# Two half-masked key blocks merged before the softmax, parted after the transpose; the pooling groups in every second step

## What is computed

```python
u_pool, q, k, v, gate_pool, gate_attn = jnp.split(hn @ w_in[l], SPLITS, axis=-1)
y_pool = pool_mixer(u_pool, pool_w_grp[l], pool_scale[l], w_pool_proj[l])
attn = swa_attention(q, k, v, sinks[l])            # 16 heads of 64, 4 key heads
merged = sigmoid(gate_pool) * y_pool + sigmoid(gate_attn) * (attn @ w_attn_proj[l])
h = h + rmsnorm(merged @ w_o[l], g[MIX_POST])
...
band_ok = (dist >= 0) & (dist < WINDOW) & (k_pos >= FRONT_PAD)     # WINDOW = 128
logits = concat([s_band - slope * dist where band_ok, s_meta, sink])
probs = softmax(logits); out = probs_band @ v + probs_meta @ v_meta
```

## Time and profile before

| | |
|---|---|
| time, median of 3 (range) | 1172.51 us (1171.82 to 1173.37) |
| the profiled execution's own time | 1172.02 us |
| its span, first to last instruction | 1170.2 us |
| TensorE busy | 1160.6 us, 99% |
| VectorE busy | 734.0 us, 63% |
| ScalarE busy | 554.6 us, 47% |
| GpSimd busy | 430.2 us, 37% |
| mean granted TensorE clock | 0.998 |

### The profile page before, as it was taken

How to read it: one execution, slowest core, us unless ns; L and a number is a source line. 1 busy time by engine, 2 the same in 40 slices (tenths; PEclk the granted TensorE clock), 3 DMA queues, 4 the chain that set the end, 5 groups by cost and what they waited for, 6 DMA issues and landing times.

```text
span 1170.2 us, 23880 instructions
## 1 busy us (share of the span) xinstructions
PE 1160.6 (99%) x9269; PEld 1133.2 (97%) x9269; DVE 734.0 (63%) x1145; ACT 554.6 (47%) x818; POOL 430.2 (37%) x486
## 2 busy tenths in 40 slices
PE   9999999999999999999999999999999999999997
PEld 8999999999999999999999999999999999999986
DVE  7655546968566865544586555459676668755542
ACT  7433335637554643333554333355376546543441
POOL 1945500007211286541109645000073122965500
PEclk9999999999999999999999999999999999999999
DMA  8854458372365365535646553573733753654540
GB/s 289 265 180 157 148 176 235 116 233 80 91 178 183 109 207 182 176 122 182 210 131 203 185 165 125 189 227 118 251 92 91 197 164 121 221 198 161 192 168 36
DMA packets 197934, 197.58 MB, mean 169 GB/s; under 512 B 4448, under 2 KB 191200, under 8 KB 197856
## 3 DMA queue, kind: packets, MB, share of 16 engines
q1 hardware_dynamic: 197712, 196.44, 53.3%
q10 hardware_dynamic: 144, 0.05, 0.0%
HBM read 195.43 MB, written 1.05 MB: 168 GB/s over the span
## 4 chain that ended last, share of the span: by engine, by line
PE 92%; issue 3%; DVE 2%; ACT 1%; DMA 0%; POOL 0%; SPq 0%; DVEq 0%; ACTq 0%; POOLq 0%
PE bank L563 27%; PE bank L565 27%; PE bank L564 27%; PE bank L826 2%; PE bank L828 2%; PE bank L827 2%; DVE w_lo L1347 1%; PE bank L915 1%; PE bank L910 1%; PE bank L869 1%; PE bank L599 1%; PE bank L598 1%; PE bank L880 1%; PE bank L626 0%; PE bank L872 0%
## 5 line engine op out<-in xcount | busy, mean ns | idle before, releaser
L563 PE MATMUL bank<-x_hi,w_hi 128*128 128x272 f32 (+1 forms) x1991 | 573.3, 288 | 0.8 <-DVE w_lo L1756 0.7
L565 PE MATMUL bank<-x_hi,w_lo 128*128 128x272 f32 (+1 forms) x1991 | 567.4, 285 | 0.0
L564 PE MATMUL bank<-x_lo,w_hi 128*128 128x272 f32 (+1 forms) x1991 | 566.3, 284 | 0.0
L1027 ACT ACTIVATE w_hi<-raw 128x2048 fp32r<-128x2048 f32 (+3 forms) x201 | 339.1, 1693 | 403.1 <-PE bank L565 383.5
L1347 DVE TENSOR_TENSOR w_lo<-raw,w_hi 128x2048 fp32r<-128x2048 f32 (+3 forms) x203 | 421.4, 2081 | 142.5 <-ACT w_hi L1027 142.2
L563 PEld LDWEIGHTS bank<-x_hi,w_hi 128*128 128x128 f32 x1991 | 374.9, 188 | 2.0 <-issue 1.2
L564 PEld LDWEIGHTS bank<-x_lo,w_hi 128*128 128x128 f32 x1991 | 375.6, 189 | 0.3
L565 PEld LDWEIGHTS bank<-x_hi,w_lo 128*128 128x128 f32 x1991 | 374.9, 188 | 0.0
L1968 POOL TENSOR_TENSOR hid_hi<-silu,up_r 128x272 f32 x88 | 142.1, 1615 | 149.3 <-DVE up_r L1543 143.2
L565 PE MATMUL bank<-hid_hi,w_lo 128*128 128x272 f32 x528 | 151.3, 287 | 0.0
L563 PE MATMUL bank<-hid_hi,w_hi 128*128 128x272 f32 x528 | 151.3, 287 | 0.0
(11 more groups left out here) (219 smaller groups left out, 1323.4 us busy)
## 6 DMA issues: line engine op xcount, KB each, us to landing
raw<-in_ffn_w_in SPq DMA_DIRECT2D x84, 1024.0 KB, 5.1
raw<-in_w_in SPq DMA_DIRECT2D x24, 1024.0 KB, 5.6
raw<-in_ffn_w_out SPq DMA_DIRECT2D x24, 768.0 KB, 4.2
raw<-in_ffn_w_out SPq DMA_DIRECT2D x24, 640.0 KB, 3.9
raw<-in_ffn_w_out SPq DMA_DIRECT2D x10, 1024.0 KB, 5.0
raw<-in_w_in SPq DMA_DIRECT2D x16, 512.0 KB, 5.4
raw<-in_w_attn_proj SPq DMA_DIRECT2D x32, 256.0 KB, 4.5
raw<-in_w_o SPq DMA_DIRECT2D x8, 1024.0 KB, 5.5
```

Of the source, the lines that this page charges most:

```text
L563: pe.matmul(ps[:, t0:T], w[0], a_hi[:, t0:T], start=start, stop=False)
L564: pe.matmul(ps[:, t0:T], w[0], a_lo[:, t0:T], start=False, stop=False)
L565: return pe.matmul(ps[:, t0:T], w[1], a_hi[:, t0:T], start=False, stop=stop)
L1027: last = act.activation(hi, w, ACT.Copy)
```

## The change

- The mask is laid on as before, and then VectorE takes, for the second block's queries, the minimum of the two key blocks' columns (they are held negated, so a masked entry is very large): one square of 128 by 128 in place of two half masked ones. `biased` is now incremented by this instruction; a new semaphore `banded` stands between.
- ScalarE's first exponential and GpSimd's first product take 144 and 128 columns in place of 272 and 256.
- `turn_p` makes two transposes of 128 by 128 in place of three, and `take_pT` copies 256 columns in place of 384.
- GpSimd, behind `pT_ready`, parts the turned square into the own block's and the earlier block's triangle with two `affine_select` (`cut_triangles`), and increments the new `pT_cut`. `attend` waits for `pT_cut` in place of `pT_ready`.
- The transposes of `p_meta` and of the spread values take 64 columns and not 128, those of the meta tokens' values 16; in layer 1 the latter are left out, with their copy.
- The pooling group g: window and mix in step 2g, group and take_z in step 2g+1. `attend_meta` moves from step 6 to step 7.

```diff
@@ turn_v
-                for j in range(2):
-                    pe.transpose(pTm_bank[:, j * P:(j + 1) * P], vT[:, j, 0:P], ident[:, :])
+                if meta_queries(l):
+                    for j in range(2):
+                        pe.transpose(pTm_bank[0:META, j * P:(j + 1) * P], vT[:, j, 0:META], ident[:, :])
@@ turn_p
-                pe.transpose(pT_bank[:, P:2 * P], s[:, META:META + P], ident[:, :])
-                last = pe.transpose(pT_bank[:, 2 * P:3 * P], s[:, META + P:T], ident[:, :])
+                last = pe.transpose(pT_bank[:, P:2 * P], s[:, META:META + P], ident[:, :])
...
-                    last = pe.transpose(pTm_bank[:, 0:P], p_meta[:, c:c + P], ident[:, :])
+                    last = pe.transpose(pTm_bank[0:4 * META, 0:P], p_meta[:, c:c + 4 * META], ident[:, :])
@@ attend
-                pe.wait_ge(pT_ready, l * HEADS + pair[1] + 1)
+                pe.wait_ge(pT_cut, l * HEADS + pair[1] + 1)
@@ TensorE's step
-                    if 1 <= c <= GROUPS:
-                        group(c - 1, l)
+                    if c % 2 == 1:
+                        group(c // 2, l)
@@ exps, take_pT
-                act.activation(s[:, 0:T], s[:, 0:T], ACT.Exp, scale=-1.0, bias=st[:, 2:3], accum_out=st[:, 4:5])
+                both = s[:, 0:META + P]
+                act.activation(both, both, ACT.Exp, scale=-1.0, bias=st[:, 2:3], accum_out=st[:, 4:5])
...
-                last = act.activation(pT[:, i % 2, :], pT_bank[:, 0:3 * P], ACT.Copy)
+                last = act.activation(pT[:, i % 2, 0:2 * P], pT_bank[:, 0:2 * P], ACT.Copy)
@@ bias_and_max
-                last.then_inc(biased, 1)
+                    if b == 0:
+                        last.then_inc(banded, 1)
+                dve.wait_ge(banded, n)
+                dve.tensor_tensor(s[:, META:META + P], s[:, META:META + P], s[:, META + P:T], ALU.min).then_inc(biased, 1)
@@ VectorE's step
-                    if 1 <= c <= GROUPS:
-                        take_z(c - 1, l)
+                    if c % 2 == 1:
+                        take_z(c // 2, l)
...
-                    if c < GROUPS:
-                        mix(c, l)
+                    if c % 2 == 0:
+                        mix(c // 2, l)
@@ GpSimd
+            def cut_triangles(i, l):
+
+                pool.wait_ge(pT_ready, l * HEADS + i + 1)
+                before, own = pT[:, i % 2, P:2 * P], pT[:, i % 2, 2 * P:3 * P]
+                pool.affine_select(out=own, in_=before, compare_op=ALU.is_ge, fill=0.0, base=0, pattern=[[1, P]],
+                                   channel_multiplier=-1)
+                pool.affine_select(out=before, in_=before, compare_op=ALU.is_ge, fill=0.0, base=-1, pattern=[[-1, P]],
+                                   channel_multiplier=1).then_inc(pT_cut, 1)
...
+                    if c % 2 == 0:
+                        g = c // 2
...
+                        window(g, l)
+                    if c >= 1:
+                        cut_triangles(2 * c - 2, l)
                     normalise(2 * c, l)
+                    if c >= 1:
+                        cut_triangles(2 * c - 1, l)
                     normalise(2 * c + 1, l)
+                cut_triangles(HEADS - 2, l)
+                cut_triangles(HEADS - 1, l)
@@ constants
-META_STEP = 6
+META_STEP = 7
```

More of the change, by code:

```diff
@@ L366, in trunk @@
         pT_ready = sem("pT_ready")
+        pT_cut = sem("pT_cut")
+        banded = sem("banded")
         o_done = sem("o_done")
@@ L846, in turn_v @@
                         pe.transpose(pT_bank[:, b * KV_DIM + j * P:b * KV_DIM + (j + 1) * P], vT[:, j, blk], ident[:, :])
-                for j in range(2):
-                    pe.transpose(pTm_bank[:, j * P:(j + 1) * P], vT[:, j, 0:P], ident[:, :])
+                if meta_queries(l):
+                    for j in range(2):
+                        pe.transpose(pTm_bank[0:META, j * P:(j + 1) * P], vT[:, j, 0:META], ident[:, :])
                 pe.wait_ge(v_spread, l + 1)
                 for j in range(2):
-                    last = pe.transpose(pTm_bank[:, KV_DIM + j * P:KV_DIM + (j + 1) * P], vT_pair[:, j, :], ident[:, :])
+                    last = pe.transpose(pTm_bank[0:4 * META, KV_DIM + j * P:KV_DIM + (j + 1) * P], vT_pair[:, j, 0:4 * META],
+                                        ident[:, :])
                 last.then_inc(v_turned, 1)
@@ L1274, in _ @@
                                ).then_inc(v_ready, 1)
-                act.activation(v_pair[:, :, :], pTm_bank[0:4 * META, KV_DIM:2 * KV_DIM].rearrange("p (j c) -> p j c", j=2),
-                               ACT.Copy)
-                act.activation(v_meta[:, :], pTm_bank[0:META, 0:KV_DIM], ACT.Copy).then_inc(v_ready, 1)
+                last = act.activation(v_pair[:, :, :], pTm_bank[0:4 * META, KV_DIM:2 * KV_DIM].rearrange(
+                    "p (j c) -> p j c", j=2), ACT.Copy)
+                if meta_queries(l):
+                    last = act.activation(v_meta[:, :], pTm_bank[0:META, 0:KV_DIM], ACT.Copy)
+                last.then_inc(v_ready, 1)
                 for u in range(46, 49):
@@ L1999, in normalise @@
                 pool.wait_ge(inv_ready, l * HEADS + i + 1)
-                for b, keys in ((1, s[:, 0:T]), (0, s[:, T:BAND])):
+                for b, keys in ((1, s[:, 0:META + P]), (0, s[:, T:BAND])):
                     inv = st[:, 1 - b:2 - b]
@@ L2018, in _ @@
                 for c in range(KD):
[L2019 to L2023, removed]
+                    if c % 2 == 0:
+                        g = c // 2
+                        pool.wait_ge(tile_read, l * TILES + T_POOL + g + 1 + TR0)
+                        if g >= 1:
+                            pool.wait_ge(mixed_ready, l * GROUPS + g)
+                        window(g, l)
+                    if c >= 1:
+                        cut_triangles(2 * c - 2, l)
                     normalise(2 * c, l)
+                    if c >= 1:
+                        cut_triangles(2 * c - 1, l)
                     normalise(2 * c + 1, l)
+                cut_triangles(HEADS - 2, l)
+                cut_triangles(HEADS - 1, l)
                 for m in range(KD):
```

## The result

The changed kernel takes 1176.08 us (median of 9, 1175.44 to 1177.04), the kernel before 1172.37 us in the same runs (median of 9). The ratio is 1.0033, with a 95% interval of 1.0024 to 1.0041: slower by 0.33%, 3.7 us. The forecast was 1173.5 us with a range of 1171.0 to 1176.5: inside the range, 2.6 us above the point, and on the side that I had given 0.28. The wait was where it was put and as long as it was worked out; what it did to the clock was priced too low, and a second, short wait was not seen.

A forecast was written before the change was run, and what follows sets the result against it. The prediction took TensorE, busy 99% of the span, to bound the kernel. Transposes -3.7, narrower transposes -0.5, wait +3.7 and clock +1.5 us sum to +1.0 on 1172.5, so 1173.5 us, range 1171.0 to 1176.5.

The forecast's parts named there:

- the side that I had given 0.28: Whole kernel: slower than a measurement can tell from no change, above 1174.9 us; chance 0.28.
- The transposes: TensorE, both layers: 32 transposes in `turn_p` and two in `turn_v` fall away, at 0.11 us each; -3.7 us.
- 3.9 to 4.2 us less: First to last step plus `turn_v`, both layers: this much shorter with the idle and slow stretch taken out.
- The narrower transposes: TensorE: 22 remaining transposes with 64 or 16 stationary columns in place of 128 get cheaper; -0.5 us.
- The end at which the gain is 0: One end for the narrower transposes: each still costs 0.11 us; the other end gains 1.6 us.
- The wait in step 7 of layer 0: TensorE's meta queries' products wait, once, until VectorE has taken the last pooling group; +3.7 us.
- Layer 1 has no meta queries and no such wait: Layer 1: the moved groups add no TensorE wait there, so nothing was charged.
- The clock: During or just behind layer 0's wait, TensorE's clock falls from 2.4 to 1.2 GHz; +1.5 us.
- The bound of 4.0: Upper price of the clock's fall: half rate for two stretches of 4.0 us loses 4.0 us.
- The cut: GpSimd's two selects before each attend, about 0.6 us, fit 1.96 us of room; no time charged.
- the rival: GpSimd's cut slips behind VectorE's split and TensorE waits, some 2.9 us an attend, slower; chance 0.12.
- The sum: Whole kernel: transposes, narrower transposes, wait and clock together +1.0 us, giving 1173.5 us.

The follow-up runs named there:

- Run 3: The changed kernel with the pooling groups in their old steps and the meta queries' products back in step 6; 1168.84 us, ratio 0.9970.
- run 9: The changed kernel with the meta queries' products behind step 7's second gate tile and VectorE's `take_z` directly behind the biases; 1169.65 us, ratio 0.9971.
- run 1: The changed kernel with the meta queries' products and their taking behind the second gate tile of layer 0's step 7; 1170.9 us, ratio 0.9981.
- run 2: The kernel before with only the pooling groups moved to every second step and the meta queries' products to step 7; 1178.51 us, ratio 1.0051.
- run 4: The changed kernel with 24 unused products into a free bank ahead of the waiting meta queries' products; 1172.85 us, ratio 1.0004.
- run 8: Run 3's kernel with one more affine select and two short waits in every cut; 1177.49 us, ratio 1.0045.
- run 5: The changed kernel with VectorE's `take_z` moved ahead of `invert_sum` and `take_o`; 1172.81 us, ratio 1.0003.
- run 7: The changed kernel with eight unused products in step 1 of layer 1, 0.93 us of added TensorE work; 1177.06 us.

## Why the prediction was right and wrong, point by point

- **The transposes**: -3.7 us forecast, by two starts 0.11 us apart. Run 3 shows 3.5 us (2.1 to 4.9). Right. The pieces show a little less: up to the last attend, layer 0 gives 1.7 us in each of runs 3 and 9, layer 1 gives 1.3 and 1.7 in place of 2.0. So the sign "3.9 to 4.2 us less" did not come: it is 3.0 and 3.4, half a microsecond less because the narrower transposes are worth nothing, and the rest is the open 0.3 us and, in run 3, the thin room of the cuts. A step without a group in layer 0 takes 8.78 us (274.25 to 283.03), where 8.77 was forecast.
- **The narrower transposes**: -0.5 us forecast, 0 measured (0.24 us to the next product's second part in both widths). Wrong: the 0.035 us of the earlier trace rows belong to products that move 16 columns, and with 128 moved columns the narrower stationary side changes nothing. The end at which the gain is 0 was the right one.
- **The wait in step 7 of layer 0**: 3.7 us forecast, 3.6 to 3.7 measured, from the chain bias, minimum, exponentials, sum, `take_o`, `take_z`. Right, and runs 1 and 2 show it from both sides.
- **"Layer 1 has no meta queries and no such wait"**: wrong. The first pool unit waits for the same four groups. The group's product ends 3.7 us ahead of `z_lo`, and one gate tile and a turn are only some 3.1 us, which leaves 0.6. The wait view lists 0.3 of it. I had looked for the wait where the code was moved, and not at every place that waits for that semaphore.
- **The clock**: that it falls was right. The price of +1.5 us fits one short fall (1.6 us, run 4 against the changed kernel's layer 0), but of the two profiled executions of the changed kernel one has a second fall and the other a fall of twice the length, and run 4 puts the share of the median at 3.2 us. This term was mis-sized by 1.7 us and carries most of the miss. The bound of 4.0 in the text held it.
- **The cut**: no slip in the changed kernel, as forecast; run 8 shows the rival to be real, at its price. The room ahead of the attends was read at one place of layer 0 (1.3 us); the least in the changed kernel is 0.5 us, in layer 1, which the prediction did not look at.
- **The sum** with the terms as measured: -3.5 + 3.7 + 0.6 + 3.2 = +4.0 us, where 3.7 were measured. The 3.2 come from the changed kernel's own median, so the sum tests the other three: they give run 4 +0.8 us, and its interval is -0.6 to +1.5.
- **The range**: the three misses (0.5, 0.6 and 1.7 us) all point the same way, so none hid another; the time lies 0.4 us inside the upper end.

## What to carry to other kernels

When a step is delayed, look up every wait on its semaphore, also far behind, and count the work that stands between. A stall of TensorE like those here (2.2 to 3.6 us) is to be priced with the half rate that may follow it: it did behind six of the seven such waits in the profiles, and cost 1.6 or 2.6 us each time. Useless products in the gap were cheaper than the gap. And separate a change of two halves before judging it: the merging alone was worth 0.3%, and one piece in the wrong place hid it.

## What the runs showed of the hardware that I had not expected

- TensorE at half rate for 3.4 us in one profile and 6.8 in another behind the same 3.6 us wait, so that one kernel's loss from one wait was 1.6 or 2.6 us.
- A fall behind a wait of 2.2 us (run 5) and none behind one of 2.99 us (run 8), and falls at layer 1's norm, where TensorE's longest gap is about 0.75 us, in 2 of the 12 profiles. Whether the second kind depends on anything in the program was not settled.
- A stationary operand of 64 columns made a transpose no cheaper than one of 128.
- A 128 by 128 affine select costs GpSimd 0.25 us to the next start, and it is held by VectorE's splits of 2.3 and of 1.2 us, as the product of the earlier trace rows is.
- A stretch of 112 us in which TensorE's products took 1% longer at a granted clock of 1.00, in one profile of twelve (run 7).
